# A Hyena mixer's spectra and output factors worked on inside PSUM, its middle filter tap on ScalarE, and two loads swapped

## Time and profile before

| | |
|---|---|
| median of three runs | 3343.19 us |
| the profiled execution: device time | 3342.78 us |
| its span (first to last instruction) | 3341.0 us |
| TensorE busy | 3185.9 us, 95% |
| VectorE busy | 1682.4 us, 50% |
| ScalarE busy | 1095.8 us, 33% |
| GpSimd busy | 1567.1 us, 47% |
| mean granted TensorE clock | 0.98 |
| mixer H: first projection matmul to the end of its out projection | 2682.81 to 2940.02 us |

### The profile page before, as it was taken

How to read it: one execution, slowest core, us unless ns; L and a number is a source line. 1 busy time by engine, 2 the same in 40 slices (tenths; PEclk the granted TensorE clock), 3 DMA queues, 4 the chain that set the end, 5 groups by cost and what they waited for, 6 DMA issues and landing times.

```text
span 3341.0 us, 39177 instructions
## 1 busy us (share of the span) xinstructions
PE 3185.9 (95%) x16114; PEld 2624.7 (79%) x16114; DVE 1682.4 (50%) x2163; ACT 1095.8 (33%) x1437; POOL 1567.1 (47%) x1138
## 2 busy tenths in 40 slices
PE   6999999999999999999999799999999999989998
PEld 5988878787878788789887677766888776668886
DVE  5763575757483443444546466665212378642213
ACT  3221243434343332332222334444222332142222
POOL 3544465546372554444433411136544566344543
PEclk9999999999999999999999899999999999989999
DMA  4544421212121332345444111102332242122331
GB/s 145 174 164 139 139 99 64 76 64 76 52 76 58 95 101 89 99 144 169 147 159 136 51 39 39 51 26 89 100 101 90 87 139 76 63 64 90 100 101 63
DMA packets 279316, 320.04 MB, mean 96 GB/s; under 512 B 6866, under 2 KB 245089, under 8 KB 278946
## 3 DMA queue, kind: packets, MB, share of 16 engines
q1 hardware_dynamic: 240960, 247.48, 23.1%
q10 hardware_dynamic: 38178, 70.06, 6.2%
HBM read 311.22 MB, written 6.29 MB: 95 GB/s over the span
## 4 chain that ended last, share of the span: by engine, by line
PE 85%; DVE 8%; ACT 3%; issue 1%; POOL 1%; DMA 1%; ACTq 0%; SPq 0%; DVEq 0%
PE ps L523 24%; PE ps L525 24%; PE ps L524 23%; PE psx L940 2%; PE psx L714 1%; PE ps L972 1%; PE psx L523 1%; PE psx L524 1%; PE psx L525 1%; PE ps L758 1%; PE psx L692 1%; PE psx L731 1%; POOL Wl L330 1%; ACT Wh L1188 1%; PE psx L659 1%
## 5 line engine op out<-in xcount | busy, mean ns | idle before, releaser
L330 POOL TENSOR_TENSOR Wl<-Wr,Wh 128x512 fp32r<-128x512 f32 x928 | 1279.0, 1409 | 1538.7 <-ACT Wh L1188 1538.6
L523 PE MATMUL ps<-Ah,Wh 128*128 128x512 f32 x2016 | 814.4, 404 | 31.8 <-DVE Al L1760 15.1
L525 PE MATMUL ps<-Ah,Wl 128*128 128x512 f32 x2016 | 788.6, 391 | 0.0
L524 PE MATMUL ps<-Al,Wh 128*128 128x512 f32 x2016 | 788.5, 391 | 0.0
L1188 ACT ACTIVATE Wh<-Wr 128x2048 fp32r<-128x2048 f32 x232 | 442.9, 1909 | 364.4 <-DMA Wr<-in_w_mlp_in_dram 109.8
L523 PEld LDWEIGHTS ps<-Ah,Wh 128*128 128x128 f32 x2016 | 380.9, 189 | 127.5 <-issue 39.9
L524 PEld LDWEIGHTS ps<-Al,Wh 128*128 128x128 f32 x2016 | 381.0, 189 | 87.5 <-issue 10.3
L525 PEld LDWEIGHTS ps<-Ah,Wl 128*128 128x128 f32 x2016 | 380.2, 189 | 81.0
L523 PE MATMUL ps<-Yh,Wh 128*128 128x512 f32 x1088 | 426.5, 392 | 4.3 <-DVE Yl L1811 4.1
L524 PE MATMUL ps<-Yl,Wh 128*128 128x512 f32 x1088 | 424.6, 390 | 0.0
L525 PE MATMUL ps<-Yh,Wl 128*128 128x512 f32 x1088 | 424.5, 390 | 0.0
(11 more groups left out here) (356 smaller groups left out, 3892.9 us busy)
## 6 DMA issues: line engine op xcount, KB each, us to landing
Wr<-in_a_w_in_dram SPq DMA_DIRECT2D x48, 1024.0 KB, 6.6
modw<-in_w_mod_dram ACTq DMA_DIRECT2D x96, 512.0 KB, 5.5
Wr<-in_b_w_in_dram SPq DMA_DIRECT2D x40, 1024.0 KB, 5.1
Wr<-in_w_mlp_in_dram SPq DMA_DIRECT2D x32, 1024.0 KB, 5.7
Wr<-in_w_mlp_out_dram SPq DMA_DIRECT2D x32, 1024.0 KB, 5.1
Wr<-in_a_w_out_dram SPq DMA_DIRECT2D x16, 1024.0 KB, 5.3
Wr<-in_c_w_in_dram SPq DMA_DIRECT2D x16, 1024.0 KB, 5.7
Wr<-in_attn_w_qkv_dram SPq DMA_DIRECT2D x12, 1024.0 KB, 5.1
```

The source lines that it names most:

```text
L330: last = pool.tensor_tensor(E.Wl[:, s, part], E.Wr[:, s, part], E.Wh[:, s, part].bitcast(F32), ALU.subtract)
L523: pe.matmul(o, ah, bh, start=first, stop=False)
L524: pe.matmul(o, ah, bl, start=False, stop=False)
L525: return pe.matmul(o, al, bh, start=False, stop=last)
```

## The change

1. **Middle tap.** ScalarE writes w1 * p + (w1 * b_in + b) straight out of the PSUM bank into the tap's destination, with a second `activation` per projection tile, before it copies the tile to `uH`. VectorE's `tensor_scalar` goes; 24 of each. The constants w1 * b_in + b are made once by two VectorE operations of 24 columns at the mixer's start. ScalarE waits for w of two tiles before where it writes into `tmp`.
2. **Spectra.** `product` sums, multiplies and adds in the two even banks themselves, so that each of its operations has one operand in PSUM; only the two sine products go to SBUF. There are 14 operations as before, and one wait more on VectorE's own results. The even banks are given back with the event ys (the end of `product`) in place of pre.
3. **Output factors.** bias * w and x0 are applied in the bank that the transform back left; ScalarE and VectorE make `Yh` and `Yl` from the bank. The banks of `back(0, n)` become 5, 7, 4, 6, and a bank is given back only with `Yl`.
4. **Loads.** On ScalarE's queue the two halves of `tabI` are asked for before the two of `kS11`.

```diff
--- before.py
+++ after.py
@@ -203,6 +203,7 @@
     E.ones, E.ident = sb("ones", [P, P]), sb("ident", [P, P])
     E.PK = sb("PK", [P, NCOL])
     E.mod = sb("mod", [P, 112])
+    E.tapH = sb("tapH", [P, 32])
     E.GC = sb("GC", [P, 2, 5, KD])
     E.sc2 = sb("sc2", [P, KD, 2])
     E.eps = sb("eps", [P, 2])
@@ -269,6 +270,11 @@
 
     t = (2, 10, 5, 13)[n]
     return E.fY[:, t:t + 3, :]
+
+
+def back_bank(half, n):
+
+    return n if half else (5, 7, 4, 6)[n]
 
 
 def filtered(E, half, fi):
@@ -1098,7 +1104,7 @@
                     into(b)
                     for k in (2 * e, 2 * e + 1):
                         m = pe.matmul(bank[b], E.tabH[:, w, k, fi * P:(fi + 1) * P], wt[:, k, :], start=(k == 2 * e), stop=(k == 2 * e + 1))
-                    emptied[b] = V.of("H", "pre", half, fi)
+                    emptied[b] = V.of("H", "pre" if e else "ys", half, fi)
             m.then_inc(*X.did("H", "f", half, fi))
 
         def back(half, n, b):
@@ -1109,7 +1115,7 @@
                         m = pe.matmul(bank[b][:, e * 256:(e + 1) * 256], filtered(E, half, fi)[:, e, w, n * P:(n + 1) * P],
                                       E.tabI[:, w, fi, e * 256:(e + 1) * 256], start=(w + fi == 0), stop=(w + fi == 2))
             m.then_inc(*X.did("H", "b", half, n))
-            emptied[b] = V.of("H", "br", half, n)
+            emptied[b] = V.of("H", "y", 0, 4 * half + n)
 
         nb = 0
         for m, part_ in H_PARTS:
@@ -1136,10 +1142,10 @@
         pe.wait_ge(*E.signals["ld_b"].of("tabI", 1))
         pe.wait_ge(*V.of("H", "ys", 0, 1))
         for n in range(4):
-            back(0, n, 4 + n)
+            back(0, n, back_bank(0, n))
         pe.wait_ge(*V.of("H", "ys", 1, 1))
         for n in range(4):
-            back(1, n, n)
+            back(1, n, back_bank(1, n))
         out("H", 0)
         post("H", False)
 
@@ -1649,11 +1655,18 @@
             act.activation(E.soH[:], so, ACT.Copy).then_inc(*A.did("H", "odd", half, fi))
 
         ahead("H", "i", 0, 0)
+        act.wait_ge(*V.of("H", "tap"))
+        act.wait_ge(*V.of("h", "H", 6))
+        act.wait_ge(*G.of("h", "H", 7))
         c = 0
         for m, part in H_PARTS:
             for f in range(2):
-                b, r = c % 4, c % 2
+                b, r, n = c % 4, c % 2, 2 * m + f
                 act.wait_ge(*T.of("H", "i", m, part, f))
+                if part and m:
+                    act.wait_ge(*V.of("H", "w", n - 2))
+                act.activation((E.x0H[:, n, :], tmp[:, f, :], tmp[:, 2 + f, :])[part], ps[b][:], ACT.Identity,
+                               bias=E.tapH[:, part * KD + n:part * KD + n + 1], scale=pk(E, "hy_w_short_2", 3 * KD + part * KD + n)).then_inc(*A.did())
                 if c >= 2:
                     act.wait_ge(*V.of("H", "ur", c - 2))
                 else:
@@ -1682,15 +1695,17 @@
                     act.dma_start(E.kS10[:, w, :, :], E.kspec[w, 0::2, :, 512:1024].rearrange("f p n -> p f n")).then_inc(*E.signals["ld_tab"].did("k", w))
         act.wait_ge(*T.of("h_end", "H"))
         for w in range(2):
+            act.dma_start(E.tabI[:, w, :, :], I["k_tabi"][w].rearrange("(k p) n -> p k n", p=P)).then_inc(*E.signals["ld_b"].did("tabI", w))
+        for w in range(2):
             act.dma_start(E.kS11[:, w, :, :], E.kspec[w, 1::2, :, 512:1024].rearrange("f p n -> p f n")).then_inc(*E.signals["ld_k"].did("k", w))
-        for w in range(2):
-            act.dma_start(E.tabI[:, w, :, :], I["k_tabi"][w].rearrange("(k p) n -> p k n", p=P)).then_inc(*E.signals["ld_b"].did("tabI", w))
         odd(1, 1)
         for half in range(2):
             for n in range(4):
                 k = 4 * half + n
                 act.wait_ge(*V.of("H", "yx", half, n))
-                act.activation(Yh[:, k, :], tmp[:, 2 + n % 2, :], ACT.Copy).then_inc(*A.did("H", "yh", k))
+                b = back_bank(half, n)
+                act.activation(Yh[:, k, :].rearrange("p (i e) -> p e i", e=2),
+                               (psx[:, b - 4, :] if b >= 4 else ps[b][:]).rearrange("p (e i) -> p e i", e=2), ACT.Copy).then_inc(*A.did("H", "yh", k))
         out("H", 0, True, E.yt, "H")
         post("H", False)
 
@@ -2227,6 +2242,10 @@
     def hyena():
         uH, x0H, wH, pwH = E.uH, E.x0H, E.wH, E.pwH
         gate("M0")
+        taps, inner, outer = (E.PK[:, COL[name] + o:COL[name] + o + 3 * KD] for name, o in (("hy_w_short_2", 3 * KD), ("hy_b_in_2", 0), ("hy_b_short_2", 0)))
+        dve.tensor_tensor(E.tapH[:, 0:3 * KD], taps, inner, ALU.mult).then_inc(*V.did())
+        dve.wait_ge(*V.now())
+        dve.tensor_tensor(E.tapH[:, 0:3 * KD], E.tapH[:, 0:3 * KD], outer, ALU.add).then_inc(*V.did("H", "tap"))
         norm("H", lambda k: GC[:, 1, 0, k:k + 1], E.Ah, E.Al)
         dve.wait_ge(*X.of("F", "k", 1, 1, 1, 1))
         for r in range(2):
@@ -2252,34 +2271,35 @@
             kc, ks = o[:, 0, 0, :], o[:, 1, 0, :]
             sums = tmp if half else E.sumH
             mr, mi = pwH[:, 0, :], pwH[:, 1, :]
-            r, i, t, u = sq[:, 0, :], sq[:, 1, :], rs[:, 0, :], rs[:, 1, :]
+            i, t = sq[:, 1, :], rs[:, 0, :]
             dve.wait_ge(*A.of("H", "odd", half, fi))
             if half + fi:
                 dve.wait_ge(*G.of("H", "mirror", *((half, 0) if fi else (0, 1))))
                 dve.wait_ge(*V.now())
             dve.tensor_tensor(sums[:, 2, :], se, so, ALU.subtract).then_inc(*V.did())
             dve.tensor_tensor(sums[:, 3, :], ce, co, ALU.subtract).then_inc(*V.did("H", "mirrored", half, fi))
-            dve.tensor_tensor(sums[:, 0, :], ce, co, ALU.add).then_inc(*V.did())
-            dve.tensor_tensor(sums[:, 1, :], se, so, ALU.add).then_inc(*V.did("H", "pre", half, fi))
+            dve.wait_ge(*V.now())
+            dve.tensor_tensor(se, se, so, ALU.add).then_inc(*V.did())
+            dve.tensor_tensor(ce, ce, co, ALU.add).then_inc(*V.did("H", "pre", half, fi))
             if half:
                 dve.wait_ge(*E.signals[("ld_tab", "ld_k")[fi]].of("k", 1))
             elif fi == 0:
                 dve.wait_ge(*E.signals["ld_h"].of(1))
             dve.wait_ge(*V.of("H", "pre", half, fi))
-            dve.tensor_tensor(r, sums[:, 0, :], kc, ALU.mult).then_inc(*V.did())
-            dve.tensor_tensor(t, sums[:, 1, :], ks, ALU.mult).then_inc(*V.did("H", "pr", half, fi))
-            dve.tensor_tensor(i, sums[:, 0, :], ks, ALU.mult).then_inc(*V.did())
-            dve.tensor_tensor(u, sums[:, 1, :], kc, ALU.mult).then_inc(*V.did("H", "pi", half, fi))
-            dve.wait_ge(*V.of("H", "pr", half, fi))
-            dve.tensor_tensor(r, r, t, ALU.subtract).then_inc(*V.did())
-            dve.wait_ge(*V.of("H", "pi", half, fi))
-            dve.tensor_tensor(i, i, u, ALU.add).then_inc(*V.did("H", "direct", half, fi))
+            dve.tensor_tensor(t, se, ks, ALU.mult).then_inc(*V.did())
+            dve.tensor_tensor(i, ce, ks, ALU.mult).then_inc(*V.did("H", "sines", half, fi))
+            dve.wait_ge(*V.of("H", "sines", half, fi))
+            dve.tensor_tensor(se, se, kc, ALU.mult).then_inc(*V.did())
+            dve.tensor_tensor(ce, ce, kc, ALU.mult).then_inc(*V.did("H", "cosines", half, fi))
+            dve.wait_ge(*V.of("H", "cosines", half, fi))
+            dve.tensor_tensor(ce, ce, t, ALU.subtract).then_inc(*V.did())
+            dve.tensor_tensor(se, se, i, ALU.add).then_inc(*V.did("H", "direct", half, fi))
             dve.wait_ge(*V.of("H", "direct", half, fi))
             dve.wait_ge(*G.of("H", "mirror", half, fi))
-            dve.tensor_tensor(o[:, 0, 0, :], r, mi, ALU.add).then_inc(*V.did())
-            dve.tensor_tensor(o[:, 1, 0, :], r, mi, ALU.subtract).then_inc(*V.did())
-            dve.tensor_tensor(o[:, 0, 1, :], i, mr, ALU.add).then_inc(*V.did())
-            dve.tensor_tensor(o[:, 1, 1, :], i, mr, ALU.subtract).then_inc(*V.did("H", "ys", half, fi))
+            dve.tensor_tensor(o[:, 0, 0, :], ce, mi, ALU.add).then_inc(*V.did())
+            dve.tensor_tensor(o[:, 1, 0, :], ce, mi, ALU.subtract).then_inc(*V.did())
+            dve.tensor_tensor(o[:, 0, 1, :], se, mr, ALU.add).then_inc(*V.did())
+            dve.tensor_tensor(o[:, 1, 1, :], se, mr, ALU.subtract).then_inc(*V.did("H", "ys", half, fi))
 
         low_banks, high_banks = [ps[b][:] for b in range(4)], [psx[:, b, :] for b in range(4)]
         c = 0
@@ -2292,8 +2312,6 @@
                 t = (x0H[:, n, :], tmp[:, f, :], tmp[:, 2 + f, :])[part]
                 tap = [pk(E, "hy_w_short_2", i * 3 * KD + part * KD + n) for i in range(3)]
                 dve.wait_ge(*A.of("H", "u", m, part, f))
-                dve.tensor_scalar(t, uH[:, r, 1:S + 1], tap[1], pk(E, "hy_b_short_2", part * KD + n), ALU.mult, ALU.add).then_inc(*V.did())
-                dve.wait_ge(*V.now())
                 dve.scalar_tensor_tensor(t, uH[:, r, 0:S], tap[0], t, ALU.mult, ALU.add).then_inc(*V.did())
                 dve.wait_ge(*V.now())
```

(14 more changed lines are left out.)

## The result

The changed kernel takes 3361.89 us (median of 5 runs, 3357.94 to 3364.68) against 3343.19 before: a ratio of 1.0052, 95% interval 1.004 to 1.0063. It is slower by 18.7 us, where 13.3 us less were forecast. The profiled execution took 3361.89 us too.

The account below looks back on a forecast made before the run. TensorE, on the chain of waits for 85% of 3341.0 us, was taken as the bound, with out waiting for the last `Yl`. That `Yl` coming 13.3 us earlier gave 3343.2 - 13.3 = 3329.9 us, range 3326 to 3338.

Parts of the forecast that it names:

- Start of the mixer: Mixer start, before the norm: two 24-column VectorE operations cost nothing, 0.5 us at most with their wait.
- B: Operations in the banks, tail, products and second transposes: at 1.78 us each, slower than before, 3352 us; chance 0.05.
- In-place writes: VectorE operations with a bank as output: 0.69 us each taken, between 0.68 and 1.78; sixteen on the tail.
- A: In-place operations, tail: 0.5 us dearer each, 8.0 us lost, about 3338 us; chance 0.13.
- Products: Each mixer product: 11.5 us in place of 14.1, GpSimd being late next.
- rival C: Mixer products: VectorE and GpSimd still slow each other with one bank operand; some 6 us gained, 3337 us; chance 0.08.
- Second transposes: TensorE's second transposes: no wait for w, 8.7 us gone together, forward(1,1) ending at 2846.8.
- Rival D: Second transposes still wait, w about 2 us late; some 4 us of gain lost, 3334 us; chance 0.09.
- Middle tap: Mixer projection tiles: 24 operations of 0.54 us leave VectorE, 24 of about 0.69 us come to ScalarE, hidden there.
- Loads: Swapped `tabI` and `kS11` loads: worth nothing or a cost of 1.2 us, `kS11` landing about 2850.5.
- Tail: Product(1,1) through the output groups: last `Yl` at 2885.8 in place of 2899.04, 13.3 us earlier.
- rival E: Shorter tail: `kS11` in time (1.2 us), TensorE keeps its clock at out's start (2 us); 3326.7 us; chance 0.05.

Follow-up runs that it names:

- the change at the old addresses: Whole change, but the tap table lies in dead columns of `mod`, so every other tensor keeps its address from the kernel before: 3329.31 us, ratio 0.9963.
- the kernel with overlapped groups: Whole change with the tap table in `mod`, plus VectorE making each `Yl` behind the next group's first operation: 3323.54 us, ratio 0.9939.

## Why the prediction was wrong, and where it held

**The step that failed** is "Start of the mixer": "Two 24-column operations on VectorE before the norm ... I cost them at nothing". As operations they are worth nothing, as VectorE's timeline of the changed kernel shows:

```profile
2702.43 0.18 DVE L2246 TENSOR_TENSOR tapH<-PK 128x24 f32<-128x24 f32 x1 [6.62 <-POOL fY L425]
2702.64 0.18 DVE L2248 TENSOR_TENSOR tapH<-tapH,PK 128x24 f32<-128x24 f32 x1
2703.20 3.35 DVE L1766 RECIPROCAL rs<-rs 128x512 f32<-128x512 f32 x1 [0.38 <-ACT rs L1216]
```

But the edit also allocates the table, and the sum had no term for a tensor's place; the table was put at nothing with a reason that covers its two operations alone. That term is 3361.89 - 3329.31 = 32.6 us. Some of it is the granted clock: of the executions with a mean of 0.98, the changed kernel took 3359.11 to 3362.38 us and the one at the old addresses 3331.52, 28 to 31 us apart, beside the 29.2 us of the table above. "From there to the end nothing changes", in the first part, failed by the same step, as what follows out is 3.7 us longer. No rival had it either: all five stood inside the mixer, B's "slower" too. The code held a sign of it: an unused tensor of 16 columns ahead of `Ah`, without which the kernel before takes 3372.03 us.

**The rest of the sum** is tested by the change at the old addresses (3329.31 us against the forecast of 3329.9; 3343.96 - 3329.31 = 14.7 us gained against 13.3). Its timelines, VectorE in product(0,0), then TensorE at the second transposes:

```profile
2775.32 0.69 DVE L2279 TENSOR_TENSOR sumH<-psx,soH 128x512 f32<-128x512 f32 x1 [4.33 <-ACT soH L1655]
...
2776.64 0.70 DVE L2282 TENSOR_TENSOR psx<-psx,soH 128x512 f32<-128x512 f32 x1
2777.25 0.69 DVE L2283 TENSOR_TENSOR psx<-psx,acc 128x512 f32<-128x512 f32 x1
...
2784.33 0.69 DVE L2299 TENSOR_TENSOR fY<-psx,pwH 128x512 f32<-128x512 f32 x1 [2.33 <-POOL pwH L476]
...
2786.72 0.74 DVE L2315 SCALAR_TENSOR_TENSOR tmp<-uH,PK,tmp 128x512 f32<-128x512 f32 x1
```
```profile
2818.98 2.07 PE L1092 MATMUL psx<-ident,wH 128*128 128x128 f32 x16
```

- *In-place writes*: 0.69 to 0.70 us with a bank as input and output, 0.69 taken. Rivals A and B are out. By the prediction's estimate from the Trainium skill (VectorE: DVE Perf Modes, section on the TRN2 errata) an operation on a bank would take 0.065 us more. The trace doesn't agree, neither for reads the earlier trace rows nor for these writes.
- *Products*: 2786.72 - 2775.32 = 11.4 us, 11.5 forecast, with VectorE waiting 2.33 us for GpSimd, as said. GpSimd's operations last 1.28 to 1.29 us beside them (up to 1.81 before): with one operand in a bank VectorE no longer slows it here, and rival C is out.
- *Second transposes*: one run of 2.07 us without a wait, the last w ready at 2816.34, and a granted clock of 1.00, the 2.4 GHz level, in the 12 us from 2818 on, against 0.50. Rival D is out. forward(1,1) ends at 2845.73, forecast 2846.8.
- *Middle tap*: free on ScalarE (0.78 us each, 0.69 forecast), as said. It was also given a share of the gain; alone it gains 3.1 us, beside the products nothing that can be measured.
- *Loads*: forecast as worth nothing or a loss of 1.2 us. Back waits 0.87 us for `tabI`, and product(1,1) waits for `kS11`, GpSimd's first operation of it standing behind a DMA:

```profile
2850.09 1.28 POOL L469 TENSOR_TENSOR pwH<-tmp,kS 128x512 f32<-128x512 f32 x1 [6.70 <-DMA kS<-kspec]
```

  2850.5 was forecast. With the old order 1.1 us come back. With overlapped groups the swap should be worth having by these numbers, which was not tried: in the old order back ends 34.0 us behind forward(1,1), and out, which the kernel with overlapped groups starts at 28.6 us, would have to follow it.
- *Tail*: the last `Yl` is ready at 2885.25, forecast 2885.8. Out ends at 2924.36, forecast 2926.7. VectorE and TensorE in the same kernel:

```profile
2884.56 0.69 DVE L2339 TENSOR_TENSOR Yl<-ps,Yh 128x512 fp32r<-128x512 f32 x1 [0.69 <-ACT Yh L1707]
```

  The first out tile starts at 2877.02, 0.1 us behind the fifth `Yl` (2876.22 + 0.69): by this timing, and since that `Yl` gives the tile its bank, it is what the "issue" wait of 2.5 us waits for; the profile doesn't name the releaser. From the last `Yl` to the end of out 39.1 us pass, against 41.0 before. Before, the granted clock was 0.50 from 2897 to 2901 us, after three stalls in out, and held up its end. Here it falls to a mean of 0.68 from 2877 to 2881 us, ahead of the wait for the last `Yl`, and is 1.00 from 2883 on. So rival E's second half, put at 2 us, came on top of the forecast, and 14.7 us were gained instead of 13.3. That 3329.31 lies only 0.6 us from the forecast is in part luck: the gain was 1.4 us larger, and the kernel before took 0.8 us more in this comparison (3343.96) than in the one that the forecast started from.

## What to carry to other kernels

A new tensor moves what is allocated behind it, and that can cost more than all its operations. Put a new small tensor last, or into columns of one that is no longer needed, and look after each edit at the mean duration of matmul groups that the edit doesn't touch. If those change, compare the places of streamed tensors and weights first (here modulo 256 bytes). Compare executions at the same mean granted clock before you explain a few us. Before costing a change, list its allocations as a part of it, and ask what an unused tensor in the code is for. In the mixer, nearly the whole gain lies in working in the banks (15.8 us by itself), and one more gain stood beside the change: overlapping the copy that VectorE waited for gave another 5.1 us in the traces. The best kernel of this study takes 3323.54 us, 0.6% less than before.

## What the runs showed of the hardware

Not expected at all: the start-to-start distance of fp32r matmuls of 512 columns depends on how far the streamed tensor stands from the weights in SBUF. It is 0.2267 us where that is a multiple of 256 bytes and 0.2324 at 128 more (from a long stretch of the mixer; the table above has the means of the whole trace). By the means of the groups without a wait: 391 ns at 0, 392 to 396 at +64, 396 to 397 at +128 and 397 at +192 (as at -64). It held for `Ah` and `Al`, for `Yh` and `Yl` (390 to 396 ns), and for `Ch` and `Cl` (389 to 395 ns). A common shift of everything by 128 bytes changed nothing.

Matmuls of 256 columns, with the weights streamed, behaved otherwise: they were 1 ns shorter at +128 and 2 to 5 ns shorter at +64 and +192. Why the chip does so, no run here shows; whether the reads of the streamed tensor meet the weight loads, or something else, was not tried.
